# A triangular inversion takes its transposed operands from VectorE's 32x32 block transposes, and the waits and loads at attention's start move to other queues

## The reference

```python
def step(state, inp):
    r_t, w_t, k_t, v_t, a_t, b_t = inp
    sa = jnp.einsum('bhvk,bhk->bhv', state, a_t)
    state = (state * w_t[:, :, None, :] + sa[..., None] * b_t[:, :, None, :]
             + v_t[..., None] * k_t[:, :, None, :])
    return state, jnp.einsum('bhvk,bhk->bhv', state, r_t)
...
merged = (jax.nn.sigmoid(gate_a) * (att @ p['w_branch_a'])
          + jax.nn.sigmoid(gate_b) * (rwkv_y @ p['w_branch_b']))
x = x + merged @ p['w_out']
x = x + jnp.square(jax.nn.relu(hm @ p['w_mlp_in'])) @ p['w_mlp_out']
```

## Time and profile before

| | |
|---|---|
| median of 3 runs | 2579.52 us (2576.33 to 2582.5) |
| the profiled execution | 2598.81 us, its span 2597.0 us |
| PE busy | 2418.4 us, 93% of the span |
| DVE / ACT / POOL busy | 1384.3 / 764.9 / 64.5 us |
| TensorE's granted clock, mean | 0.966 of full speed (2.4 GHz) |
| rwkv stage | 604.3 us, attention 344.7 us |

### The profile page before, as it was taken

One profiled execution on the slowest core, in us unless ns is written; L12 is line 12 of the kernel. 1 busy time (PEld: TensorE's weight loads), 2 busy tenths in 40 slices (PEclk: granted clock), 3 DMA queues, 4 the chain that ended last, 5 costly groups with the idle time before them and its releaser, 6 DMA issues. The chain is left out here.

```text
span 2597.0 us, 53071 instructions
## 1 busy us (share of the span) xinstructions
PE 2418.4 (93%) x22029; PEld 1817.1 (70%) x22029; DVE 1384.3 (53%) x3001; ACT 764.9 (29%) x1434; POOL 64.5 (2%) x102
## 2 busy tenths in 40 slices
PE   7999999988999989897889889999999999999998
PEld 4566788755666566665556667787888888888886
DVE  3257888954455464336566656656434533533443
ACT  3226888134143342224454532122001000100101
POOL 0020000000000000001101100000000000000000
PEclk8989999999989999899999999999999999999999
DMA  6432222361221213237778744311111111111112
GB/s 181 116 111 78 74 80 89 104 185 48 83 78 51 78 47 92 80 102 215 254 223 270 235 178 133 101 48 35 36 45 43 39 48 34 49 33 49 33 33 77
DMA packets 289420, 252.43 MB, mean 97 GB/s; under 512 B 53607, under 2 KB 240584, under 8 KB 289053
## 3 DMA queue, kind: packets, MB, share of 16 engines
q1 hardware_dynamic: 214804, 201.49, 25.0%
q10 hardware_dynamic: 74376, 47.56, 6.6%
HBM read 198.84 MB, written 48.59 MB: 95 GB/s over the span
## 5 line engine op out<-in xcount | busy, mean ns | idle before, releaser
L1286 PE MATMUL rwkv_banks<-gate_sides_then_att_T 128*128 128x384 f32 (+1 forms) x768 | 288.1, 508 | 8.2 <-PEq L441 3.7
L2947 DVE TENSOR_TENSOR x<-x,ps_mm 128x272 f32<-128x272 f32 x280 | 120.9, 436 | 308.1 <-PE ps_mm L2914 308.0
L2938 ACT COPY merged_then_hidden<-ps_mm 128x272 f32<-128x272 f32 x160 | 61.5, 385 | 720.2 <-PE ps_mm L2914 720.2
L2914 PE MATMUL ps_mm<-merged_then_hidden,w_mm 128*128 128x272 f32 x960 | 227.1, 393 | 1.6 <-DVE sums_of_right_sides_ L3167 0.9
L2914 PEld LDWEIGHTS ps_mm<-merged_then_hidden,w_mm 128*128 128x128 f32 x960 | 182.2, 190 | 39.9 <-DVE sums_of_right_sides_ L3167 1.3
L2914 PE MATMUL ps_mm<-v_T_and_gates_then_h_mlp,w_mm 128*128 128x272 f32 x864 | 204.5, 392 | 0.0
L1286 PEld LDWEIGHTS rwkv_banks<-gate_sides_then_att_T 128*128 128x128 f32 x768 | 141.3, 200 | 77.8 <-issue 20.2
L2914 PEld LDWEIGHTS ps_mm<-v_T_and_gates_then_h_mlp,w_mm 128*128 128x128 f32 x864 | 164.1, 190 | 33.9
L2914 PE MATMUL ps_mm<-sums_of_right_sides_,w_sums_mm 128*128 128x272 f32 x704 | 165.3, 392 | 1.1 <-DVE sums_of_right_sides_ L3125 1.1
L2947 DVE TENSOR_TENSOR merged_then_hidden<-merged_then_hidden,ps_mm 128x272 f32<-128x272 f32 x120 | 51.5, 434 | 195.4 <-PE ps_mm L2914 195.4
L2914 PEld LDWEIGHTS ps_mm<-sums_of_right_sides_,w_sums_mm 128*128 128x128 f32 x704 | 133.7, 190 | 29.0 <-issue 1.5
(11 more groups left out here) (512 smaller groups left out, 4125.7 us busy)
## 6 DMA issues: line engine op xcount, KB each, us to landing
v_pages<-in_cache_v SPq DMA_DIRECT2D x128, 256.0 KB, 4.8
gate_sides_then_att_T<-in_w_in ACTq DMA_DIRECT2D x46, 512.0 KB, 4.2
_and_tildes_then_k_pages<-in_cache_k SPq DMA_DIRECT2D x88, 256.0 KB, 3.3
w_mm<-in_w_mlp_in SPq DMA_DIRECT2D x32, 512.0 KB, 4.8
w_mm<-in_w_mlp_out SPq DMA_DIRECT2D x32, 512.0 KB, 5.0
w_pr<-in_w_in SPq DMA_DIRECT2D x27, 512.0 KB, 5.1
k_pages<-in_cache_k SPq DMA_DIRECT2D x40, 256.0 KB, 3.6
v_T_and_gates_then_h_mlp<-gates_T SPq DMA_DIRECT2D x16, 544.0 KB, 4.7
```

The lines of the kernel that those rows point to most:

```text
L1286: ins = MM(B[:, gate_bank(n), 0:w], gw[:, n % 2, k_, :], hc[:, k_, 0:w], start=(k_ == 0), stop=(k_ == KO - 1))
L2914: ins = self.nc.tensor.matmul(self.ps[:, c, self.BANK[step], 0:272], left[step][:, k, :], right[step][:, k, 272 * c:272 * c + 272], start= ...
L2938: self.nc.scalar.copy(self.target(step, rows, c), self.out(act, u, step, c)).then_inc(self.by_act, 1)
L2947: self.nc.vector.tensor_tensor(to, to, ps, ALU.add).then_inc(self.by_dve, 1)
```

## The change

It has five parts.

1. **Inversion.** `unfold`, `hop` s = 0 and s = 2 and `level_x` make one product instead of two (36 bursts of 32 products go over the four rounds; `level_x` with l = 1 had half a burst as its second). The other operand is made by DVE's `V.transpose`, which transposes each 32x32 block: in `keep_unfolded` and `keep_x` behind the step that makes `xt`, and in a new `turn_hop` behind ACT's copy. PE's `hop` s = 1 and `level_x` l = 0 wait for a new semaphore `x_turned`.
2. **Late gates.** ACT's `gates()` places the units from `late` on (the last rounds' tail) by 4.5 behind instead of 0.9.
3. **Attention's first loads.** The eight pieces of `near_k` are started by SP instead of ACT, and POOL waits for `near` alone.
4. **Rows of the next pair.** k and q are loaded by ACT's queue, key 2.11 i - 0.01.
5. **Keys in pairs.** PE turns page keys c and c+1 together, and ACT's key for its copy moves with it.

```diff
             def unfold(i, L):
...
-                by_quad(IB[L], 0, diagonal(L), eye)
                 by_quad(IB[L], 256, eye, diagonal(L)).then_inc(S["p_made"], 1)
             def hop(i, L, s):
                 if s == 0:
                     pe.wait_ge(S["n_kept"], i * 4 + L + 1)
-                    by_quad(IB[L], 0, of(xt, L), of(x, L))
-                    ins = by_quad(IB[L], 256, of(x, L), of(xt, L))
+                    ins = by_quad(IB[L], 0, of(xt, L), of(x, L))
                 elif s == 1:
                     pe.wait_ge(S["h_kept"], i * 4 + L + 1)
+                    pe.wait_ge(S["x_turned"], i * 4 + L + 1)
...
                 else:
                     pe.wait_ge(S["n_kept"], i * 4 + 2 + L + 1)
-                    by_quad(IB[L], 0, of(ent, L), of(pm, L))
-                    ins = by_quad(IB[L], 256, of(pm, L), of(ent, L))
+                    ins = by_quad(IB[L], 0, of(ent, L), of(pm, L))
             def level_x(i, L, l):
                 pe.wait_ge(S["p_kept"], i * 2 * LV + 2 * l + L + 1)
-                by_quad(IB[L], 0, of(xt, L), of(pm, L), range(0, 4, 1 if l < LV - 1 else 2))
+                if l == 0:
+                    pe.wait_ge(S["x_turned"], i * 4 + 2 + L + 1)
                 by_quad(IB[L], 256, of(pm, L), of(xt, L)).then_inc(S["x_made"], 1)
...
-                    yield gate_keys[n * KO + KO - 1] + (4.5 if gate_keys[n * KO] < 0 else 0.9)
+                    yield gate_keys[n * KO + KO - 1] + (4.5 if n < early or n >= late else 0.9)
...
             def keep_hop(i, L, s):
-                nc.scalar.copy(xx[:, L, :, :, :].rearrange("p a n c -> p (a n c)"), B[:, IB[L], :]).then_inc(S["h_kept"], 1)
+                nc.scalar.copy(x[:, L, :, :].rearrange("p n c -> p (n c)"), B[:, IB[L], 0:256]).then_inc(S["h_kept"], 1)
...
-                ch.done(V.tensor_tensor(xx[:, L, :, :, :], B[:, IB[L], :].rearrange("p (a n c) -> p a n c", a=2, n=8), within,
-                                        ALU.mult))
+                ch.done(V.tensor_tensor(xt[:, L, :, :], quads(IB[L], 256), each_chunk(const("within")[:, 32:64]), ALU.mult))
+                ch.mark(V.transpose(x[:, L, :, :].rearrange("p n c -> p (n c)"), xt[:, L, :, :].rearrange("p n c -> p (n c)")))
                 V.tensor_tensor(ent[:, L, :, :], xt[:, L, :, :], each_chunk(const("eye32")), ALU.add).then_inc(S["n_kept"], 1)
+            def turn_hop(i, L, s):
+                dve.wait_ge(S["h_kept"], i * 4 + s + L + 1)
+                V.transpose(xt[:, L, :, :].rearrange("p n c -> p (n c)"), x[:, L, :, :].rearrange("p n c -> p (n c)"))\
+                    .then_inc(S["x_turned"], 1)
...
             def keep_x(i, L, l):
                 dve.wait_ge(S["x_made"], i * (2 * LV + 2) + 2 * l + L + 1)
-                if l < LV - 1:
-                    to = xx[:, L, :, :, :].rearrange("p a n c -> p (a n c)")
-                    V.tensor_tensor(to, to, B[:, IB[L], :], ALU.add).then_inc(S["x_kept"], 1)
-                else:
...
-                    V.tensor_tensor(xt[:, L, :, :], xt[:, L, :, :], quads(IB[L], 256), ALU.add).then_inc(S["x_kept"], 1)
+                ch.done(V.tensor_tensor(xt[:, L, :, :], xt[:, L, :, :], quads(IB[L], 256), ALU.add))
+                V.transpose(x[:, L, :, :].rearrange("p n c -> p (n c)"), xt[:, L, :, :].rearrange("p n c -> p (n c)"))\
+                    .then_inc(S["x_kept"], 1)
...
+                        yield hop_at(i, 1) + 3.0 * L + 1.3
+                        turn_hop(i, L, 0)
...
+                        yield hop_at(i, 3) + 3.0 * L + 1.3
+                        turn_hop(i, L, 2)
...
-                        yield 2.11 * i - 0.01
-                        sp.wait_ge(S["chunk_made"], 2 * i * NCH)
-                        sp.dma_start(k[:, :], p.proj[B_K + i, :, 0:NT]).then_inc(S["in_k"], 16)
-                        sp.dma_start(q[:, :], p.proj[B_Q + i, :, 0:NT]).then_inc(S["in_q"], 16)
...
+            def near_of_sample():
+                yield 0.06
+                sp.wait_ge(S["near_zero"], 1)
+                for n in range(HA):
...
-            pool.wait_ge(S["bias_in"], 16 * (1 + HA))
+            pool.wait_ge(S["near_in"], 16)
...
-                        for c in range(HP):
+                        for c in range(0, HP, 2):
                             yield b + 0.2 * j + 0.05 * c
                             turn_keys(b, j, c)
+                            turn_keys(b, j, c + 1)
...
-                        yield b + 0.2 * j + 0.05 * c + 0.001
+                        yield b + 0.2 * j + 0.05 * (c - 1) + 0.001
...
+            def next_pair():
+                for i in range(1, HP):
+                    yield 2.11 * i - 0.01
+                    act.wait_ge(S["chunk_made"], 2 * i * NCH)
+                    act.dma_start(k[:, :], p.proj[B_K + i, :, 0:NT]).then_inc(S["in_k"], 16)
+                    act.dma_start(q[:, :], p.proj[B_Q + i, :, 0:NT]).then_inc(S["in_q"], 16)
```

More of the change, by code:

```diff
@@ L1110, in rwkv @@
              "round_made", "gn_mean", "gn_sub", "gn_sq", "gn_var", "gn_kept", "gn_root", "a_made", "a_kept", "n_kept", "h_kept", "p_made", "p_kept",
-             "x_made", "x_kept", "shifted", "v_mixed", "xw_kept", "turned", "rows_kept", "av_made", "av_kept", "wx_made", "wx_kept",
+             "x_made", "x_kept", "x_turned", "shifted", "v_mixed", "xw_kept", "turned", "rows_kept", "av_made", "av_kept", "wx_made", "wx_kept",
              "e_made", "rp_kept", "mi_kept", "nf_kept", "y0_kept", "s_made", "s_kept", "y1_made", "y1_kept", "so_made",
@@ L2024, in keep_x @@
                 dve.wait_ge(S["x_made"], i * (2 * LV + 2) + 2 * l + L + 1)
-                if l < LV - 1:
-                    to = xx[:, L, :, :, :].rearrange("p a n c -> p (a n c)")
-                    V.tensor_tensor(to, to, B[:, IB[L], :], ALU.add).then_inc(S["x_kept"], 1)
-                else:
-                    for e in range(2):
-                        q = Q[2 * e]
-                        ch.mark(V.tensor_tensor(x[q, L, :, :], x[q, L, :, :],
-                                                B[q, IB[L], 0:256].rearrange("p (n c) -> p n c", n=8), ALU.add))
-                    V.tensor_tensor(xt[:, L, :, :], xt[:, L, :, :], quads(IB[L], 256), ALU.add).then_inc(S["x_kept"], 1)
+                ch.done(V.tensor_tensor(xt[:, L, :, :], xt[:, L, :, :], quads(IB[L], 256), ALU.add))
+                V.transpose(x[:, L, :, :].rearrange("p n c -> p (n c)"), xt[:, L, :, :].rearrange("p n c -> p (n c)"))\
+                    .then_inc(S["x_kept"], 1)
             def keep_ends(i, g):
@@ L2165, in rounds @@
                     for L in range(2):
+                        yield hop_at(i, 1) + 3.0 * L + 1.3
+                        turn_hop(i, L, 0)
+                    for L in range(2):
                         yield hop_at(i, 2) + 3.0 * L + 1.0
                         keep_fourth(i, L)
+                    for L in range(2):
+                        yield hop_at(i, 3) + 3.0 * L + 1.3
+                        turn_hop(i, L, 2)
                     for l in range(LV):
@@ L2270, in attention @@
     NTURN, NP, NCH = len(turns), len(turns) - 6, P_BEFORE[NI]
-    names = ("bias_in", "near_zero", "in_q", "in_k", "in_v", "scaled", "chunk_made", "chunk_kept", "kept", "mixed",
+    names = ("bias_in", "near_in", "near_zero", "in_q", "in_k", "in_v", "scaled", "chunk_made", "chunk_kept", "kept", "mixed",
              "exped", "turned", "turn_kept", "diag", "out_made", "out_kept", "rows_out", "dve",
@@ L2361, in masks @@
                         sp.dma_start(mk[32 * c:32 * c + 16, :], p.msk_d[b]).then_inc(S["mk_in"], 16)
-            weave(prompt(), keys(), values(), masks(), new_rows())
+            def near_of_sample():
+                yield 0.06
+                sp.wait_ge(S["near_zero"], 1)
+                for n in range(HA):
+                    r0 = 32 * (n // 2) + ST * (n % 2)
+                    sp.dma_start(p.near_k[r0:r0 + ST, :],
+                                 bass.AP(p.bias_d.tensor, n * head + 127, [[NW - 1, ST], [1, 128 + ST]]))\
+                        .then_inc(S["bias_in"], 16)
+            weave(prompt(), keys(), values(), masks(), new_rows(), near_of_sample())
             sp.wait_ge(S["rows_out"], 64 * HP)
@@ L2579, in _ @@
             act.dma_start(p.near[:, :, :], bass.AP(p.bias_d.tensor, 127, [[NW - 1, 128], [head, HA], [1, 256]]))\
-                .then_inc(S["bias_in"], 16)
-            act.wait_ge(S["near_zero"], 1)
-            for n in range(HA):
-                r0 = 32 * (n // 2) + ST * (n % 2)
-                act.dma_start(p.near_k[r0:r0 + ST, :],
-                              bass.AP(p.bias_d.tensor, n * head + 127, [[NW - 1, ST], [1, 128 + ST]]))\
-                    .then_inc(S["bias_in"], 16)
+                .then_inc(S["near_in"], 16)
             def keep_turned(i, key):
@@ L2773, in mask @@
                     if b == 0:
-                        dve.wait_ge(S["bias_in"], 16 * (1 + HA))
+                        dve.wait_ge(S["bias_in"], 16 * HA)
                     tail = X[:, W - 128:W]
```

3 lines of the change are left out of this document (1 added, 2 removed).

## The result

The change is faster: 2539.65 us (2535.67 to 2542.7, 4 runs) against 2577.93 us for the kernel before (2576.17 to 2582.5, 4 runs), ratio 0.9831, 95% interval 0.9807 to 0.9856. That is 38.3 us by the medians. The forecast was 2528 with 2506 to 2558 around it, 51.5 us less.

The account below looks back on a forecast made before the run. PE's own time was taken to bound the rwkv and attention stages. Terms -23 - 15 - 7 + 1.5 - 2 - 4 - 3 gave -52.5 us; less a microsecond, 2579.5 - 51.5 = 2528 us, range 2506 to 2558.

Parts of the forecast that it names:

- The bursts: Inversion in the rwkv stage: 36 bursts removed from PE at 0.64 us each save 23 us (21 to 26.5).
- The stalls: Line 1372 in the rwkv stage: 15 of 23.7 us of PE's waits for late instructions go (0 to 23.7).
- The first rival: Inversion: only the bursts' own time comes back, stalls move to remaining bursts, clock stays 0.92; 2549 us, chance 0.22.
- The clock: PE in the rwkv stage: fewer stalls mean fewer half-clock spells, saving 7 us (0 to 20).
- The transposes: VectorE's 40 new transposes at 0.45 us: PE waits 0.4 us between levels in each of 4 rounds, +1.5 us.
- rivals 3 and 4: Inversion: PE waits for VectorE's chain, 2555 to 2574 us, chance 0.06; transposes exceed the hops' cover, 2610 us, chance 0.03.
- The end of the stage: End of the rwkv stage: y is done sooner but the last gate store still ends it, saving 2 us (0 to 3).
- The start of attention: Attention's first loads: POOL can begin its masks near 1190.5 instead of 1194.17, saving 4 us (2 to 6).
- Rows of the next pair: Attention's pair boundaries: earlier issue by ACT gains 3.5 us at the first; 3 us saved in all (0 to 5).
- Key turns in pairs: Attention's key turns on PE: pairing changes an order in which PE waited a microsecond or two, 0 us (-3 to +3).
- The sum: Whole kernel: terms total -52.5 us, cut to 51.5 off the 2579.5 us median, giving 2528 us; chance 0.58.

Follow-up runs that it names:

- e4: The change, with two wide products (256 and 80 columns, results unread) in place of each of the 36 removed bursts: ratio 0.9859 to the kernel before, mean 2547.4 us.
- e1: The kernel before, unedited, timed and profiled once more over 12 runs: ratio 0.9995 to the kernel before, mean 2585.0 us.
- e6: The change, with the 36 removed bursts computed again and their results unread: ratio 0.9964 to the kernel before, mean 2579.4 us.
- e7: The change, with every transpose made twice on VectorE: ratio 0.9817 to the kernel before, mean 2545.4 us.
- e8: The change, with hop 1's second burst written behind the next gate products: ratio 0.9806 to the kernel before, mean 2540.8 us.
- e12: The change, with hop 1's second burst behind the next gate products and one 256-column product per quad in unfold: ratio 0.9767 to the kernel before.
- e9: The kernel before with only attention's first loads changed; one execution, profile only: attention stage 343.7 us against 348.2 and 349.6.
- e10: The kernel before with only k and q of the next pair moved to ACT's queue; one execution, profile only: attention stage 334.8 us.
- e11: The kernel before with only the key turns made in pairs; one execution, profile only: attention stage 345.0 us.

## Why the prediction was right, step by step

**The bursts, -23.** L1372 lost 25.0 us of busy time, between the 23 and the 26.5. As a saving of time it was less, and this term was mis-sized: e4 puts that much PE time back and loses 13.5 us at equal clock, since PE waits for instructions again once it has less to do between them.

**The stalls, -15.** 14.6 on L1372, and e1 shows that they hardly vary between executions. The first rival (only the bursts' own time comes back, 2549) is refuted by e6 against e4. That the stalls are late instructions, which the prediction argued from the counts, is borne out by the landings on q8. Two things it passed over: not all "issue" waits were on L1372 (2.8 us of before's stood on L1470 and L1420), and those elsewhere grew to 4.8, so that PE's idle time in the stage fell by 9.6 us and not by 14.6. The Trainium skill ("Runtime: NRT & Kernel Launch", section "Instruction fetch mechanics") states that crossing a block of instructions is mostly hidden. This trace does not agree for its bursts: 23.7 us of waits on L1372 before, which end behind the landings of such blocks.

**The clock, -7.** Over the timed runs the mean clock rose from 0.9713 and 0.9695 to 0.9732, which at 2.03 us per 0.001 is 4 to 7.5. The mechanism that I gave for it, that each stall is followed by a spell of half clock, is not shown: e6 has before's stalls and 0.9713, but e7 and e8, with the change's stalls or fewer, have 0.9703. For it speaks that e4 and e12, with the fewest stalls (1.8 and 4.4 us), have the highest means, 0.9763 and 0.976. It stays open.

**The transposes, +1.5.** 0.44 us each where 0.45 was taken from bounds of 0.42 and 1.82; 1.8 us of waits on keep_x, though at `last_p` and not between levels 0 and 1. e7 refutes rivals 3 and 4. The Trainium skill ("Vector Engine (DVE) Microarchitecture Reference", section 3.8) states one element per cycle and lane for a transpose. That fits 445 ns for 256 columns, beside 421 for a sum of as many; no run here has a second size to show the pace itself.

**The end of the stage, -2.** 4.94 to 2.80 at the barrier: 2.1.

**The start of attention, -4.** 2.7 from barrier to the 256-column products. The mask came sooner, but `near` was not there as early as the step took it to be, and the copy of the keys now waits behind `q_new_T`. Over the whole stage no gain can be told (e9's idle time, 48.2 us, is within the 45.5 to 50.8 of the kernels without this part), so the term was too large.

**Rows of the next pair, -3.** This term was mis-sized the other way: 8.3 us of waits went in e10. The step took the 6.6 us from issue to use as fixed and counted only the earlier issue. But SP had started four page loads (3.65 us of issues) just before it, and behind ACT's queue the same transfer was used 4.2 us after its issue (1253.38 to 1257.59). The 2.69 us at the second boundary fell to 1.3, where I had nothing. That the page loads ahead are what held the transfer up is argued from this comparison, not shown by a run of its own.

**Key turns in pairs, 0.** No gain in waits in e11.

**The sum.** The rwkv stage was forecast near 557 us and took 561.7 and 549.7 in two profiles, attention near 338 and took 332.9 and 336.2. At equal clock the change is 41 us below the kernel before, and the better clock adds 4 to 7.5: 45 to 48.5, against 51.5 forecast and 38 and 49 measured, whose intervals overlap. What the sum had too much of is the bursts, valued one for one where part of the time became waiting (23 against 13.5), and the start of attention; what it had too little of is the pair's rows (3 against 8.3 of waits). These errors partly cancel, and that attention's parts and the late gates came to the 9 us forecast, term by term off, is luck.

## What to carry to other kernels

Count instructions, not only busy time: where very small products stand in a row, an engine can wait for its own program, and the same PE time in a sixteenth of the records was worth 22 us here. Before costing a moved transfer, ask what stood ahead of it on the old queue; its landing time there is not its own. And when a kernel's runs differ by more than its change, set the granted clock beside each time before comparing.

## What the runs showed of the hardware

A mean granted clock 0.001 higher goes with 2.03 us less in a 2580 us kernel, 0.08%, and that is most of the difference between its executions. Whether the program has a say in it is not settled: e4 and e12 had means 0.005 above the kernel before. TensorE waited for its own instructions: they came in transfers of 16 KB, 256 records each and never less than 3.2 us apart, and 157 of 160 stalls inside the bursts ended 1.1 to 1.6 us after one had landed. Four 32x32x256 products in four quads take 0.57 us together, hardly less than the 0.64 us of the 32 products of 32 columns that they replace, and near the 0.49 us that 256 columns of a gate product take (1.46 us for 2 x 384). Small products in different quads lose little in PE's time; what they cost is their number in a short time.
